# Another order of small steps in a two-block kernel: first turns of the probabilities, a filter network's second layer, and two splits

## The reference

```python
# first block (x: 512 x 1024)
h = rms_norm(x, norm_in)
dq, dk, dv, dgate, cq, ckv, kr, mgate, g_diff, g_mla = split(h @ w_in)
# four differential heads: two causal softmax maps per head, p = p0 - lam * p1
o_diff = rms_norm(causal_multimap_attention(dq, dk, dv, [1, -lam], 64 ** -0.5), diff_subln) * (1 - lambda_init)
o_diff = o_diff * silu(dgate)
# four latent heads: queries from cq (rank 384), keys and values from ckv (rank 256)
q = rms_norm(cq, mla_q_norm) @ w_uq          # 384 -> 4 * (128 + 64), the 64 are rotated
kv = rms_norm(ckv, mla_kv_norm) @ w_ukv      # 256 -> 4 * (128 + 128)
o_mla = causal attention of q and (k_nope, rotated kr) over mv
o_mla = o_mla * silu(mgate)
merged = sigmoid(g_diff) * (o_diff @ w_proj_diff) + sigmoid(g_mla) * (o_mla @ w_proj_mla)
x = rms_norm(x + merged @ w_out, norm_final)
# second block: adaln (silu(c) @ mod_w), a hyena mixer, a gated convolution network
h = sin(freq * (pos @ f_w1 + f_b1)); h = sin(freq * (h @ f_w2 + f_b2))
h = sin(freq * (h @ f_w3 + f_b3))            # the filter's network, three layers
kern = (h @ f_wout) * decay, normalised; y = fft convolution of x1 * v with kern
x = x + g1 * ((x0 * y) @ hy_w_out + b);  x = x + g2 * conv_ffn(modulate(rmsnorm(x), sh2, sc2))
```

## Time and profile before

| | before |
|---|---|
| median of 3 runs (lowest to highest) | 1042.02 us (1041.53 to 1042.57) |
| the profiled execution | 1041.58 us |
| its span, first to last instruction | 1039.4 us |
| PE busy | 1027.0 us, 99% |
| DVE busy | 738.0 us, 71% |
| ACT busy | 413.7 us, 40% |
| POOL busy | 573.1 us, 55% |
| mean granted clock of TensorE | 0.999 |

### The profile page before, as it was taken

The page is one execution under the profiler, slowest core; times in us unless marked ns, Lnnn a source line. Parts: engine busy times, 40 slices in busy tenths (PEclk is TensorE's granted clock), DMA queues, the critical chain, the costliest instruction groups (busy, mean ns, idle before and its releaser), DMA issues.

```text
span 1039.4 us, 13302 instructions
## 1 busy us (share of the span) xinstructions
PE 1027.0 (99%) x4886; PEld 847.7 (82%) x4886; DVE 738.0 (71%) x1053; ACT 413.7 (40%) x681; POOL 573.1 (55%) x420
## 2 busy tenths in 40 slices
PE   9999999999999999999999999999999999999997
PEld 7889887777878888778888888778888888888886
DVE  7768957756878667994888968686666666671563
ACT  4233646665545244743444342533232223231222
POOL 2896996999410064545544276534655546574542
PEclk9999999999999999999999999999999999999999
DMA  8755364432665722404332223312222322223222
GB/s 343 289 199 201 117 212 148 107 137 92 212 172 198 295 109 81 162 14 108 123 122 81 102 84 145 117 65 98 81 81 81 135 107 81 81 81 128 115 81 81
DMA packets 21996, 136.91 MB, mean 132 GB/s; under 512 B 3973, under 2 KB 4405, under 8 KB 15288
## 3 DMA queue, kind: packets, MB, share of 16 engines
q1 hardware_dynamic: 9360, 94.74, 24.4%
q0 software_dynamic: 8224, 31.73, 9.9%
q10 hardware_dynamic: 4358, 9.72, 2.5%
HBM read 128.83 MB, written 6.31 MB: 130 GB/s over the span
## 4 chain that ended last, share of the span: by engine, by line
PE 83%; POOL 5%; DVE 5%; DMA 4%; ACT 2%; issue 1%; SPq 0%; ACTq 0%; POOLq 0%; DVEq 0%
PE bank L526 70%; PE bank L517 7%; DMA arena<-mod_w_in 4%; POOL arena L1819 2%; PE bank L532 2%; POOL arena L1817 1%; PE bank L787 1%; PE bank L781 1%; DVE ring_parts L2025 1%; DVE arena L2178 1%; DMA ring<-weights_in 1%; PE bank L776 1%; POOL mod_part L1822 0%; PE bank L997 0%; ACT ring_parts L1224 0%
## 5 line engine op out<-in xcount | busy, mean ns | idle before, releaser
L1801 POOL TENSOR_TENSOR ring_parts<-ring,ring_parts 128x1024 fp32r<-128x1024 f32 x101 | 251.6, 2497 | 237.7 <-ACT ring_parts L1224 234.1
L526 PE MATMUL bank<-hT_parts,ring_parts 128*128 128x512 f32 x1344 | 339.0, 393 | 1.2 <-ACT hT_parts L1567 1.2
L1224 ACT ACTIVATE ring_parts<-ring 128x1024 fp32r<-128x1024 f32 (+3 forms) x165 | 168.5, 1031 | 370.2 <-PE bank L526 172.6
L526 PEld LDWEIGHTS bank<-hT_parts,ring_parts 128*128 128x128 f32 x1344 | 249.6, 188 | 54.9 <-ACT hT_parts L1567 2.8
L526 PE MATMUL bank<-ring_parts,arena_parts 128*128 128x512 f32 (+1 forms) x744 | 172.9, 384 | 1.1 <-DVE ring_parts L2025 1.1
L526 PE MATMUL bank<-ring_parts,hT_parts 128*128 128x512 f32 (+2 forms) x676 | 168.3, 377 | 0.0
L526 PEld LDWEIGHTS bank<-ring_parts,arena_parts 128*128 128x128 f32 x744 | 137.4, 188 | 28.9 <-DVE ring_parts L2025 1.3
L526 PE MATMUL bank<-arena_parts,ring_parts 128*128 128x512 f32 x592 | 147.9, 390 | 0.0
L526 PEld LDWEIGHTS bank<-ring_parts,hT_parts 128*128 128x128 f32 x676 | 123.2, 188 | 21.0 <-issue 0.2
L2701 DVE SCALAR_TENSOR_TENSOR arena<-bank,small,arena 128x441 f32<-128x441 f32 (+2 forms) x176 | 122.3, 695 | 21.0 <-DVE arena L2701 1.4
L526 PEld LDWEIGHTS bank<-arena_parts,ring_parts 128*128 128x128 f32 x592 | 111.0, 188 | 24.7 <-DVE arena_parts L2458 2.0
(11 more groups left out here) (246 smaller groups left out, 1124.6 us busy)
## 6 DMA issues: line engine op xcount, KB each, us to landing
ring<-weights_in SPq DMA_DIRECT2D x39, 2048.0 KB, 7.9
arena<-mod_w_in POOLq DMA_DIRECT2D x32, 512.0 KB, 4.1
arena<-mod_w_in POOLq DMA_DIRECT2D x8, 1024.0 KB, 9.2
x_sb<-xT_in SPq DMA_DIRECT2D x4, 512.0 KB, 6.8
ring<-weights_in SPq DMA_DIRECT2D x4, 512.0 KB, 7.5
arena<-x_in SPq DMA_DIRECT2D x4, 512.0 KB, 11.0
mod_spill<-mod_part POOLq DMA_DIRECT2D x16, 128.0 KB, 2.2
arena<-mod_spill POOLq DMA_DIRECT2D x8, 256.0 KB, 4.2
```

The source lines that it names most:

```text
L526: ins = nc.tensor.matmul(out, l, r, start=start and n == 0, stop=stop and n == len(passes) - 1)
L1224: return nc.scalar.activation(out, in_, ACT.Copy)
L1801: return nc.gpsimd.tensor_tensor(part(low), low, part(high), ALU.subtract)
```

## The change

The change does five things. (a) The third piece of `w_uq` is split on DVE in two instructions: columns 512 to 767 (the rotated ones) at the old place, columns 0 to 511 behind the two low parts of ckv; PE waits for each apart. (b) In unit 0, `fill(0)` puts the low terms of pieces 0 to 2 before `scores(1)`, and piece 3 with its low terms inside `scores(1)`; on ACT the second high part of the gate's weight moves behind `mv_out(0)`. (c) T0 and T1 of units 0 to 6 move from the head of `values(u)` into `scores(u + 1)`: ahead of the masks for a differential head, ahead of the third tile's second half for a latent one. Unit 7 keeps its place. (d) POOL makes the heads' roots one modulation step earlier, the network's second layer moves one gate tile back on PE, DVE and ACT, and DVE's second `mod_chunk` of the list one step forward. (e) Around the second norm DVE does the first `input_full` ahead of the first `taps_ab`, and the `taps_cd` stand one step later each.

```diff
-MOD_AFTER = (9, 13, 16, 17, 19)
+MOD_AFTER = (9, 12, 16, 17, 19)
-ROOTS_AFTER = (10, 20, 22, 24, 26)
+ROOTS_AFTER = (10, 19, 21, 23, 25)
-NET_AFTER = (2, 4, 7)
+NET_AFTER = (2, 5, 7)
...
                 if m == 0:
-                    pe.wait_ge(sem("piece_low"), FIRST_UQ + KQ)
+                    pe.wait_ge(sem("lat_low"), KQ + 1)
+                    pe.wait_ge(sem("piece_low"), FIRST_UQ + KQ - 1)
                 product3(bank[4 + m][:, 0:256], *pairs, start=False, terms=((0, 1),)).then_inc(sem("latq_done"), 1)
+            pe.wait_ge(sem("piece_low"), FIRST_UQ + KQ)
             for h in range(HEADS):
...
-                for a, i in tiles:
+                for n, (a, i) in enumerate(tiles):
+                    if between and n == (2 if latent else 0):
+                        between()
                     out, q, keys = place(a, i)
...
-                    if not last:
+                    if low_qs:
+                        pe.wait_ge(sem("piece_low"), FIRST_MGATE + low_qs[-1] + 1)
+                        ks = slice(2 * low_qs[0], 2 * low_qs[-1] + 2)
+                        ins = product3(bank[b], lefts[ks], rights[ks], start=False, stop=low_qs[-1] == PIECES - 1, terms=((0, 1),))
+                    if not low_qs or low_qs[-1] < PIECES - 1:
                         return
...
+            def first_turns(u):
+                turn_probs(u, 0)
+                turn_probs(u, 1)
...
-            scores(1)
-            fill(0, (PIECES - 1,))
+            fill(0, (), range(PIECES - 1))
+            def rest_and_turns():
+                fill(0, (PIECES - 1,), (PIECES - 1,))
+                first_turns(0)
+            scores(1, rest_and_turns)
             values(0)
             fill(1)
             for u in range(1, UNITS - 1):
-                scores(u + 1)
+                scores(u + 1, lambda: first_turns(u))
                 values(u)
...
+            first_turns(UNITS - 1)
             values(UNITS - 1, lambda part: gate_tile(0, part))
...
-            for m in range(2):
-                split_high(FIRST_MGATE + m)
+            split_high(FIRST_MGATE)
             mv_out(0)
+            split_high(FIRST_MGATE + 1)
             exps(0, (0,))
...
+            def split_last_uq(s):
+                p = FIRST_UQ + KQ - 1
+                wait("piece_high", p + 1)
+                low, high = piece_parts(p)
+                return V.tensor_tensor(part(low[:, s]), low[:, s], part(high[:, s]), ALU.subtract)
             for i in range(KQ + KKV):
                 if i == KQ:
-                    split_low(FIRST_UQ + KQ - 1)
+                    split_last_uq(slice(512, UQ_W)).then_inc(sem("lat_low"), 1)
...
+            split_last_uq(slice(0, 512)).then_inc(sem("piece_low"), 1)
...
             taps_even(0)
-            taps_ab(0, 0)
             for k in range(KD):
                 input_full("n2", 0, N2_BANKS, x_low, (k,))
-                if k == 0:
-                    taps_ab(0, 1)
-                if 2 <= k < 6:
-                    taps_cd(0, k - 2)
+                if k in (0, 2):
+                    taps_ab(0, k // 2)
+                if 3 <= k < 7:
+                    taps_cd(0, k - 3)
```

More of the change, by code:

```diff
@@ L704, in turn_latents @@
                 for i in ((), (), range(KQ), range(KQ, KQ + KKV))[m]:
-                    take((i + 1) % 4, "lat_low", i + 1)
+                    take((i + 1) % 4, "lat_low", i + 1 + (i >= KQ))
                     turn((i + 1) % 4, [lat[:, t, i * P:(i + 1) * P] for t in range(TT)]).then_inc(sem("lat_turned"), 1)
@@ L744, in _, with scores @@
             pe.wait_ge(sem("constants_in"), 64)
-            def scores(u):
+            def scores(u, between=None):
                 latent, h = u >= HEADS, u % HEADS
@@ L789, in scores, with fill @@
                 ins.then_inc(sem("scores_done"), 1)
-            def fill(u, qs=range(PIECES), last=True):
+            def fill(u, qs=range(PIECES), low_qs=range(PIECES)):
                 b = FILL_BANK[u]
@@ L817, in fill, with turn_probs @@
                 ins.then_inc(sem("fill_done"), 1)
+            def turn_probs(u, i):
+                b = 5 + i % 2
+                p1 = probs1[u % 2]
+                pe.wait_ge(sem("probs_ready"), 4 * u + i + 1)
+                take(b, "pT_out", 4 * u + i + 1)
+                turn(b, [p1[:, OFF[i] + j * P:OFF[i] + (j + 1) * P] for j in range(i + 1)]).then_inc(sem("p_turned"), 1)
+            def first_turns(u):
+                turn_probs(u, 0)
+                turn_probs(u, 1)
             def values(u, between=None):
                 latent, h = u >= HEADS, u % HEADS
-                p1 = probs1[u % 2]
-                def turn_probs(i):
-                    b = 5 + i % 2
-                    pe.wait_ge(sem("probs_ready"), 4 * u + i + 1)
-                    take(b, "pT_out", 4 * u + i + 1)
-                    turn(b, [p1[:, OFF[i] + j * P:OFF[i] + (j + 1) * P] for j in range(i + 1)]).then_inc(sem("p_turned"), 1)
                 def weigh(i):
@@ L877, in _ @@
                 if m == TT - 1:
-                    fill(0, range(PIECES - 1), last=False)
+                    fill(0, range(PIECES - 1), ())
                 tokens = slice(m * P, (m + 1) * P)
```

10 lines of the change are left out of this document (3 added, 7 removed).

## The result

The changed kernel takes 1048.85 us by median (1048.44 to 1050.02, 4 runs), beside 1042.23 for the kernel before (4 runs): ratio 1.0067, interval [1.0054, 1.0079], slower. Forecast were 1045.3 and a range to 1047.9. The direction was right, the size half of the measured one, and the time lies outside the range.

The account below looks back on a forecast made before the run. PE was taken as the bound, busy 1027.0 of 1039.4 us. The terms sum to +1.26, giving 1042.84, or 1043.3 on the median's scale; the clock's fall adds 2.0, making 1045.3, range 1041.5 to 1047.9.

Parts of the forecast that it names:

- Queries' split: PE's wait for DVE's third piece of the queries' split: a smaller part ends sooner beside POOL's instruction, -0.54 us.
- Unit 0: PE's 0.6 us wait for ACT ahead of the first W, mostly covered by the masks' row, -0.34 us net.
- Units 1 to 6 and the heads' roots: Turns moved inside scores hide ACT's copy of T0, -2.48 us; earlier POOL roots are not on PE's path, 0.
- Second layer, first place: Network's second-layer product, one gate tile later, no longer waits for the sine nor loses pipeline overlap, -0.39 us.
- Third place: Third layer's product: PE waits for the second layer's sine, now behind two sigmoids and a table load on ACT, +5.62 us.
- The clock: TensorE's clock falls to half in the wait before the third layer's product, costing 2.0 us, ends 0 and 2.6.
- Second norm: DVE's full tile comes 0.6 us earlier ahead of taps_ab, so PE's wait for it goes, -0.61 us.

Follow-up runs that it names:

- The filled wait: The changed kernel with five more 128x512 matmuls, on a bank that nobody reads, on PE ahead of the third layer's product: 1045.63 us, ratio 1.0038.

## Why the prediction was wrong, point by point

*Queries' split* (forecast -0.54, measured -0.70): mechanism and size right. The 256-column part started at 130.36, POOL's 128x1024 instruction at 130.51, and the part took 2.36 us: it was held for POOL's whole instruction, as the 128x768 one of the earlier trace rows was:

```profile
130.36 2.36 DVE L2201 TENSOR_TENSOR ring_parts<-ring,ring_parts 128x256 fp32r<-128x256 f32 x1
130.51 1.91 POOL L1831 TENSOR_TENSOR arena<-arena,stat 128x1024 f32<-128x1024 f32 x1
```

The combine's 4.53 and 4.72 us, in place of 2.2, are of the same kind. The Trainium skill, page "SBUF — State Buffer", section "🔬 SBUF: two separate sides", gives the port pair to whichever of the two starts first; in these rows DVE starts 0.15 us ahead of POOL and is the one that waits, so the exclusive holding agrees and the order of precedence doesn't show in the recorded starts.

*Unit 0* (forecast -0.34, measured 0): the first W's wait shrank from 0.62 to 0.17. The product's wait for ACT's moved high part took back 0.28 of it (its matmuls at 160.17 start 0.73 us behind the two before them, in place of 0.45), and about 0.16 more went in places that no view names. The forecast named the wait, and was too low for what goes against it. (`fill(0)` has 12 matmuls for pieces 0 to 2, not 16; nothing in the sum hangs on it.)

*Units 1 to 6 and the heads' roots* (forecast -2.48 and 0, measured -0.13 together): here a step failed. The gain per unit is right: the timeline of unit 1 shows the masks now between the turns and the first W, without a gap,

```profile
180.29 0.55 PE L532 MATMUL bank<-small,arena 128*128 128x128 f32 x3
180.67 0.61 PE L792 MATMUL bank<-masks 128*128 128x128 bf16 x8
181.12 0.44 PE L517 MATMUL bank<-arena 128*128 128x128 f32 x2
```

and units 1, 2, 4, 5 and 6 give 0.30 to 0.40 each. But the prediction wrote that "PE's next use of the head's output lies two units later". Counted from the head's values that is so, but POOL and DVE finish the output in that same later round, shortly before PE turns it. In the trace of before DVE ends it at 210.49 and PE turns it at 212.05, 1.6 us of room:

```profile
208.85 1.64 DVE L2263 TENSOR_TENSOR arena<-arena 128x512 f32<-128x512 f32 x1
212.05 0.60 PE L532 MATMUL bank<-small,arena 128*128 128x128 f32 x4
```

In the changed kernel PE comes 1.2 us sooner and DVE ends 1.8 us later, behind a combine of 4.72 us in place of 2.23:

```profile
203.38 4.72 DVE L2261 SCALAR_TENSOR_TENSOR arena<-arena,sums 128x128 f32<-128x128 f32 x4
205.64 1.91 POOL L1831 TENSOR_TENSOR arena<-arena,stat 128x1024 f32<-128x1024 f32 x1
212.37 0.66 PE L532 MATMUL bank<-small,arena 128*128 128x128 f32 x4 [1.39 <-DVE arena L2285]
```

Unit 3 lost 1.7 in all. The wait of 3.50 in the earlier trace rows was read as DVE's own; it was the sign that POOL, not PE, sets the pace of that output. The traces of the experiments show what each part is worth, as the change of PE's lead over the trace of before, from unit 0's first W to the first gate tiles (one execution each):

| turns moved | list of the roots | from, to | change |
|---|---|---|---|
| no | 19, 21, 23, 25 | -0.16, +0.51 | +0.67 |
| units 1 to 6 only | 20, 22, 24, 26, as before | -0.44, -0.03 | +0.41 |
| yes, network's lists as before | 20, 22, 24, 26, as before | +0.10, +1.24 | +1.14 |
| yes (the changed kernel) | 19, 21, 23, 25 | -0.68, -0.82 | -0.14 |
| yes, sine and MOD_AFTER as before | 19, 21, 23, 25 | -0.27, -0.38 | -0.11 |
| yes, sine and MOD_AFTER as before | 19, 22, 23, 25 | -1.31, -2.97 | -1.66 |

So neither edit gives anything alone. Without earlier roots the turns give nothing, with the second head's roots at the wrong step unit 3 gives the gain back, and with that one step put right two thirds of the forecast 2.48 us are there.

*Second layer, first place* (forecast -0.39, measured -0.29): right; in other runs the same product waits 0.7, 1.2 and 1.4, so the edit covers a wait that varies with what DVE has behind it.

*Third place* (forecast +5.62, measured +6.23): mechanism right, and the clock time of the sine's end too (forecast PE's start at 316.7, measured 316.59). The forecast's chain was to come earlier with PE; PE's lead was small, and the 6.1 is what remained.

*The clock* (forecast +2.0 with ends 0 and 2.6, measured +3.2): the fall came, and here a size failed: the upper end was too low. It was taken from ten matmuls at the program's start, and the slow stretch lasts longer than these: 7.0 us behind the wait. (That the view prints a clock of 1.00 over those first matmuls says nothing: the trace holds no clock record before 7.4 us.) The 5.0 us between the last matmul and the fall, on which the forecast weighed its chances, was one draw: in the fourteen traces this time runs from 2.1 to 5.2 us. In the changed kernel the fall came 2.9 us into the wait, and a wait of 4.4 was enough too, so the weighing of 5.6 against 5.0 us was no good guide, and that the fall came as forecast was in part luck. The filled wait measures the term by itself, 3.2. The Trainium skill, page "TensorE: Matmul & The Clock Gate", section "HAM oscillation — how this bites in real kernels", has the group behind an idle gap start cold; the trace agrees, with 3.78 us for eight matmuls that take 1.98 elsewhere.

*Second norm* (forecast -0.61): measured -0.61.

Put together, the forecast's +3.3 lacked 2.35 in the units, 0.34 in unit 0, 0.6 at the wait and 1.2 at the clock, less 0.16 and plus 0.1 for the rest: 7.7, the 7.72 by which the last matmul is late (the two profiled executions differ by 7.58). The direction came out right because the wait at the third product was forecast by its true mechanism; the size was lost in the units first, then in the clock.

## What to carry to other kernels

When a bound engine is made faster by tenths of a microsecond a round, look first which other engine hands it something once a round, and how much room that has at its smallest; a long wait of the helper engine for a third one says that the third sets the pace. Before moving one small step later, list on each engine what now stands ahead of it between its input and its use: here 4.5 of 6.1 us came from ACT's order, which put the wait for tile 6's scale, two sigmoids and a table load ahead of the sine. List too what the moved step sets free: a turn moved later kept DVE from a buffer. A wait on TensorE costs its length and can cost the clock behind it: in the one case tried here, where the wait was left, useless matmuls in it gave 3.2 us back.

## What the runs showed of the hardware

The granted clock's fall is not tied to one length of idle time. Counted from PE's last matmul ahead of a wait, it came after 2.9 us (wait 6.1), 5.1 us (wait 6.5), 4.9 us (wait 4.4) and 2.9 us (wait 1.6). In the last two PE had already resumed, 0.5 and 1.3 us before. Other waits passed without a fall: 1.25 us and 1.42 us at the second layer's product, and 1.64 us behind the filling matmuls. The work done at the low clock lasted 7.0, 5.5, 3.4 and 3.4 us, and half of that is the price by the rates (3.5, 2.7, 1.7 and 1.7 us); for the first, 3.2 was measured. Ten executions of the one kernel with a wait of 1.6 spread over 6.7 us. Why it falls in some and not in others stays open.

In the places shown, a DVE instruction with two SBUF inputs beside POOL's 128x1024 instruction of 1.9 us took about that time on top of its own: 2.36 us for a 128x256 subtraction, 2.89 for a 128x768 one that takes 0.94 elsewhere. No trace says which of the two the hardware served first.
